# Gather rings of six and eight slots, a row-tiled spread, query and key gains ahead of the root, and new interleaving tables in a two-layer decoder step

## The reference, cut to what matters

```python
def peer_block(xt):                                # 128 tokens
    q = (xt @ w_q).reshape(128, 8, 2, 128)
    s1, s2 = q[:, :, 0] @ keys0.T, q[:, :, 1] @ keys1.T
    ...                                            # top 16 of the sums of two top 16: idx, top
    g = softmax(top)
    act = gelu(einsum('thkd,td->thk', u_tab[idx], xt))   # dots
    return einsum('thk,thkd->td', g * act, v_tab[idx])   # value sum

def mla_in(h, pos):                                # queries and keys of layer 0
    z = h @ w_in
    cq, ckv, kr = rms_norm(z[:256]), rms_norm(z[256:384]), z[384:]
    q = rope_tail(rms_norm((cq @ w_uq).reshape(8, 96), g_q), pos)
    k = rope_tail(rms_norm(concat(ckv @ w_uk, kr), g_k), pos)
```

## Time and profile before

| what | value |
| --- | --- |
| median of 3 runs | 2081.88 us (2077.25 to 2082.18) |
| the profiled execution, its own time | 2065.61 us |
| its span, first to last instruction | 2063.8 us |
| PE busy | 1503.8 us, 73% |
| DVE busy | 1321.5 us, 64% |
| POOL busy | 1203.5 us, 58% |
| data moved | 751.57 MB, 364 GB/s over the span |

### The profile page before, as it was taken

The page is one execution under the profiler, slowest core; times in us unless marked ns, Lnnn a source line. Parts: engine busy times, 40 slices in busy tenths (PEclk is TensorE's granted clock), DMA queues, the critical chain, the costliest instruction groups (busy, mean ns, idle before and its releaser), DMA issues.

```text
span 2063.8 us, 25764 instructions
## 1 busy us (share of the span) xinstructions
PE 1503.8 (73%) x9294; PEld 737.5 (36%) x9294; DVE 1321.5 (64%) x3189; ACT 355.2 (17%) x934; POOL 1203.5 (58%) x1097
## 2 busy tenths in 40 slices
PE   5775558774657869987886889978888871455667
PEld 2454223631233425552542447524543320111212
DVE  1459977699776645348889854478899417543452
ACT  1200122120121211111231311112122110011112
POOL 0023577476687564447767763457777437765575
PEclk8898788887767879898898888988888885678788
DMA  9859899999889999899999999899999889999999
GB/s 364 343 194 411 286 368 363 402 415 366 334 308 379 344 355 403 329 368 397 346 378 379 361 377 392 328 367 330 386 386 362 332 343 348 393 421 417 419 399 374
DMA packets 213942, 751.57 MB, mean 364 GB/s; under 512 B 27237, under 2 KB 35629, under 8 KB 213817
## 3 DMA queue, kind: packets, MB, share of 16 engines
q0 software_dynamic: 155136, 564.20, 71.3%
q1 hardware_dynamic: 58680, 185.72, 23.1%
HBM read 747.74 MB, written 2.10 MB: 363 GB/s over the span
## 4 chain that ended last, share of the span: by engine, by line
PE 24%; DVE 16%; DMA 13%; POOL 6%; issue 4%; ACT 1%; SPq 0%; POOLq 0%; DVEq 0%; ACTq 0%
PE yacc L1259 7%; DVE uring L2031 4%; DMA vring<-in_peer_v,expert 4%; POOL uring L798 3%; POOL vring L798 3%; DMA uring<-in_peer_u,expert 3%; DMA wring<-in_sg_w_in 3%; PE pp L1047 2%; PE pp L1021 2%; DMA wring<-in_peer_w_q 1%; DVE arena L1914 1%; PE pp L1110 1%; PE ps L1145 1%; PE pq L1110 1%; DMA wring<-in_sg_w_out 1%
## 5 line engine op out<-in xcount | busy, mean ns | idle before, releaser
L798 POOL DMA_INDIRECT uring<-in_peer_u,expert x512 | 577.0, 1127 | 462.2 <-DVE dots L2031 184.2
L1259 PE MATMUL yacc<-vring,diag 64*64 64x512 f32 x4096 | 621.9, 723 | 274.0 <-DMA vring<-in_peer_v,expert 147.9
L798 POOL DMA_INDIRECT vring<-in_peer_v,expert x512 | 553.9, 1082 | 355.2 <-PE yacc L1259 237.1
L2031 DVE CUSTOM_DVE_ANT_0 uring<-uring,h 128x1024 f32<-128x1024 f32 x512 | 613.7, 1225 | 205.3 <-DMA uring<-in_peer_u,expert 197.1
L1259 PEld LDWEIGHTS yacc<-vring,diag 64*64 64x64 f32 x4096 | 147.6, 154 | 606.5 <-issue 324.4
L1551 ACT ACTIVATE diag<-cst,wts 128x64 f32<-128x64 f32 (+1 forms) x528 | 155.4, 339 | 442.7 <-PE yacc L1259 367.2
L1047 PE MATMUL pp<-hT,wring 128*128 128x128 f32 x1024 | 128.2, 288 | 11.4 <-DMA wring<-in_peer_w_q 8.3
L1047 PEld LDWEIGHTS pp<-hT,wring 128*128 128x128 f32 x1024 | 124.0, 202 | 27.1 <-issue 16.4
L1914 DVE TENSOR_REDUCE arena<-arena 128x16 f32<-128x1024 f32 x64 | 77.9, 1217 | 20.8 <-ACT arena L1490 20.0
L1110 PE MATMUL pp<-w_uk,arena 128*128 128x512 f32 x128 | 76.8, 690 | 8.9 <-ACT arena L1490 8.9
L1111 PEld LDWEIGHTS ps<-qabs,arena 128*128 128x128 f32 x256 | 51.1, 200 | 66.4 <-issue 66.4
(11 more groups left out here) (306 smaller groups left out, 1824.3 us busy)
## 6 DMA issues: line engine op xcount, KB each, us to landing
wring<-in_peer_w_q SPq DMA_DIRECT2D x48, 1024.0 KB, 12.9
wring<-in_sg_w_in SPq DMA_DIRECT2D x48, 768.0 KB, 8.7
wring<-in_w_mod SPq DMA_DIRECT2D x35, 1024.0 KB, 9.5
wring<-in_sg_w_out SPq DMA_DIRECT2D x18, 1024.0 KB, 10.4
uring<-in_w_mod SPq DMA_DIRECT2D x9, 1024.0 KB, 11.9
wring<-in_mla_w_o SPq DMA_DIRECT2D x9, 1024.0 KB, 10.4
uring<-in_peer_u,expert POOLq DMA_INDIRECT x512, 7.1
vring<-in_peer_v,expert POOLq DMA_INDIRECT x512
```

Source lines behind the costliest of these rows:

```text
L798: pool.indirect_dma_start(ring[:, slot % RING, :], None, table[n // 3], bass.IndirectOffsetOnAxis(ap=idx, axis=0)).then_inc(land[slot % RI ...
L1259: last = pe.matmul(yacc[64 * q:64 * q + 64, r], diag[at, slot % RING, :], v[at, 512 * q:512 * q + 512], start=first, stop=final)
L2031: dve.tensor_tensor_reduce(u, u, rows_h[:, :], 1.0, 0.0, ALU.mult, ALU.add, dots[:, p % 2, i:i + 1]).then_inc(u_used, 1)
```

## The change

- `uring` gets 6 slots and `vring` 8; together they stay 14. The number of chunks loaded ahead stays six.
- `spread` reads only the 32 partitions of each quarter, so that a matmul takes a quarter of PE's rows. It runs in two turns; a turn takes quarters that lie in different row groups and writes different PSUM banks. Between the turns PE waits for the first turn's matmuls on a new semaphore. `norm` spreads its two rows together.
- `rsqrt_column` takes the place of `rsqrt` in `norm` and in the value norm of the sgu stages (`norm_v`). It is given minus half of the mean, and a round takes two instructions instead of three, so 8 in place of 11.
- In `mla_in` DVE now reads queries and keys from PSUM, multiplies them by the gains and rotates them before the root; ACT squares from PSUM at the same time and makes no copy. After the root one multiplication is left.
- All five tables are new. There are fewer spots on DVE, so the numbers aren't comparable one by one.

```diff
-RING = 7
+URING, VRING = 6, 8
 WRING = 4
-AHEAD = 2 * (RING // 2)
+AHEAD = 6
...
 PLAN_PE = """
-178:VV 179:NVVNNNNVNVV 180:VVV 181:VVVVV 186:V 189:VVV 191:V 193:VVVVV 194:V 200:VNV 206:VVVVVVV 209:VV 212:V 225:VV
...
+160:VVVVV 162:V 164:V 166:V 172:VVV 181:VVVV 187:V 190:VVV 191:V 192:VVVV 193:V 200:VV 205:V 206:VVVVVVV 209:VV 217:V
...
 PLAN_POOL = """
-UUUUUUVUUVVUUUUUVUUUVVUUUUUVUUUVVUVVUVVVUVVUVUVVVUUUUVVVUUUUUUUUVVVUUUUVVUVUVUUUVUUUVUVUUVVVUUVUUVUUUUUUVUUVUUUVUUUV
...
+UUUUUVUUVUVUUVUUUUUVUVVUUUVUUVVVUVVVUVUUVUUUVUVUUUUUVVUUUUUVUVVUUUVVUUVVVVUUVVVUUUUUUUUVVUUVVUUVUVVUUUVUUVUUUUUUVUUU
...
     if kind == "mla_in":
-        return ["z", "cT", "qk"], ["c", "kr", "qk"], ["z", "cT", "qk", "sq"]
+        return ["z", "cT", "qk"], ["c", "kr", "keys", "gain", "qk"], ["z", "cT", "queries", "sq"]
...
-            def gather(slot, ring, table, used, land):
+            def gather(slot, ring, size, table, used, land):
...
-                if slot >= RING:
-                    pool.wait_ge(used, slot - RING + 1)
+                if slot >= size:
+                    pool.wait_ge(used, slot - size + 1)
...
             def tables(k):
-                after(pe, ACTE, k - 1, "qk")
+                after(pe, ACTE, k - 1, "sq")
+                after(pe, DVE, k - 1, "gain")
...
-                spread(pp, mod_row(k) + 1)
-                signal(spread(pss, mod_row(k)), "rows")
+                signal(spread((pp, mod_row(k) + 1), (pss, mod_row(k))), "rows")
...
-            def spread(out, r):
-
-                pe.wait_ge(mod_done[DVE], mod_count(r))
-                for q in range(4):
-                    one = 32 * q + NT
-                    last = pe.matmul(out[:, q // 2, 256 * (q % 2):256 * (q % 2) + 256],
-                                     ident[:, one:one + 1].to_broadcast([P, P]), mrows[:, r, :], start=True, stop=True)
+            def spread(*rows):
+
+                for out, r in rows:
+                    pe.wait_ge(mod_done[DVE], mod_count(r))
+                for turn in range(2):
+                    for i, (out, r) in enumerate(rows):
+                        for bank in range(2):
+                            q = 2 * bank + (turn + i) % 2
+                            at, one = slice(32 * q, 32 * q + 32), 32 * q + NT
+                            last = pe.matmul(out[:, bank, 256 * (q % 2):256 * (q % 2) + 256],
+                                             ident[at, one:one + 1].to_broadcast([32, P]), mrows[at, r, :], start=True, stop=True)
+                            if turn == 0:
+                                last.then_inc(spread_half, 1)
+                                halves[0] += 1
+                    if turn == 0:
+                        pe.wait_ge(spread_half, halves[0])
                 return last
...
-                z, cT, qk, sq = (shape_of(tile, a, b) for a, b in ((z_, z_s), (cT_, cT_s), (qk_, qk_s), (sq_, sq_s)))
+                z, cT, sq = (shape_of(tile, a, b) for a, b in ((z_, z_s), (cT_, cT_s), (sq_, sq_s)))
                 after(act, PE, k, "z")
                 signal(copy(z[0:r, :], ps[0][0:r, 0:416]), "z")
                 point(k, 0)
                 after(act, PE, k, "cT")
                 signal(copy(cT[:, 0:3 * r], ps[1][:, 0:3 * r]), "cT")
+                keys = sq[0:r, 768:1536].rearrange("p (h d) -> p h d", h=H)
+                after(act, DVE, k, "kr")
+                act.activation(keys[:, :, NOPE:QK], krt[tile][0:r, :].unsqueeze(1).to_broadcast([r, H, ROPE]), ACT.Square)
                 after(act, PE, k, "qk")
-                copy(qk[0:r, 0:480], pp[0:r, 0, 0:480])
-                copy(qk[0:r, 480:768], pp[0:r, 1, 0:288])
-                keys = qk[0:r, 768:1536].rearrange("p (h d) -> p h d", h=H)
-                signal(copy(keys[:, :, 0:NOPE], ps[0][0:r, :].rearrange("p (h d) -> p h d", h=H)), "qk")
-                after(act, ACTE, k, "qk")
-                after(act, DVE, k, "kr")
-                signal(act.activation(sq[0:r, :], qk[0:r, :], ACT.Square), "sq")
+                act.activation(sq[0:r, 0:480], pp[0:r, 0, 0:480], ACT.Square)
+                signal(act.activation(sq[0:r, 480:768], pp[0:r, 1, 0:288], ACT.Square), "queries")
+                after(act, DVE, k, "keys")
+                signal(act.activation(keys[:, :, 0:NOPE], ps[0][0:r, :].rearrange("p (h d) -> p h d", h=H), ACT.Square), "sq")
...
-                if slot >= RING:
-                    act.wait_ge(v_used, slot - RING + 1)
+                if slot >= VRING:
+                    act.wait_ge(v_used, slot - VRING + 1)
...
+            def rsqrt_column(out, negative_half, tmp):
+
+                link(ts(out.bitcast(U32), negative_half.bitcast(U32), 1, None, ALU.logical_shift_right))
+                link(ts(out.bitcast(U32), out.bitcast(U32), -1.0, COLUMN_MAGIC, ALU.mult, ALU.add))
+                for _ in range(3):
+                    link(stt(tmp, out, out, negative_half, ALU.mult, ALU.mult))
+                    link(stt(out, tmp, 1.5, out, ALU.add, ALU.mult))
...
-                link(ts(scr[:, 0:1], ps[0][:, 0:1] if tile == S else scr[:, 0:1], 1.0 / D, EPS, ALU.mult, ALU.add))
-                rsqrt(scr[:, 1:2], scr[:, 0:1], rs[:, 0:1])
+                link(ts(scr[:, 0:1], ps[0][:, 0:1] if tile == S else scr[:, 0:1], -0.5 / D, -0.5 * EPS, ALU.mult, ALU.add))
+                rsqrt_column(scr[:, 1:2], scr[:, 0:1], rs[:, 0:1])
...
-                signal(cp(q4[:, 1, :, NOPE:QK], times(krt[tile][0:r, :], H)), "kr")
-                point(k, 0)
+                gq, gk = gqk[0:r, 0:QK], gqk[0:r, QK:2 * QK]
+                signal(tt(q4[:, 1, :, NOPE:QK], times(krt[tile][0:r, :], H), times(gk[:, NOPE:QK], H), ALU.mult), "kr")
+                point(k, 0)
+                after(dve, PE, k, "qk")
+                signal(tt(q4[:, 1, :, 0:NOPE], ps[0][0:r, :].rearrange("p (h d) -> p h d", h=H), times(gk[:, 0:NOPE], H),
+                          ALU.mult), "keys")
+                after(dve, ACTE, k, "queries")
+                link(tt(q4[:, 0, 0:5], pp[0:r, 0, 0:480].rearrange("p (h d) -> p h d", h=5), times(gq, 5), ALU.mult))
+                signal(tt(q4[:, 0, 5:8], pp[0:r, 1, 0:288].rearrange("p (h d) -> p h d", h=3), times(gq, 3), ALU.mult), "gain")
+                if tile == S:
+                    cos, sin = const("cos_q", r), const("sin_q", r)
+                else:
+                    cos, sin = (const(c)[:, HALF * tile:HALF * tile + HALF] for c in ("cos_p", "sin_p"))
+                link(rotate(q3[:, :, NOPE:QK], times(cos, 2 * H), times(sin, 2 * H), rt))
                 point(k, 1)
                 after(dve, ACTE, k, "sq")
                 s16, v16 = scr[0:r, 16:32], scr[0:r, 32:48]
                 link(dve.tensor_reduce(v16, sq.rearrange("p (i d) -> p i d", i=2 * H), X, ALU.add))
                 link(ts(v16, v16, 1.0 / QK, EPS, ALU.mult, ALU.add))
                 rsqrt(s16, v16, rs[0:r, 0:16])
-                link(tt(q3, q3, over(s16, QK), ALU.mult))
-                for i in range(2):
-                    link(tt(q4[:, i], q4[:, i], times(gqk[0:r, QK * i:QK * i + QK], H), ALU.mult))
-                if tile == S:
-                    cos, sin = const("cos_q", r), const("sin_q", r)
-                else:
-                    cos, sin = (const(c)[:, HALF * tile:HALF * tile + HALF] for c in ("cos_p", "sin_p"))
-                signal(rotate(q3[:, :, NOPE:QK], times(cos, 2 * H), times(sin, 2 * H), rt), "qk")
+                signal(tt(q3, q3, over(s16, QK), ALU.mult), "qk")
...
-                link(ts(scr[:, 0:1], squares, 0.25 / SGH, EPS, ALU.mult, ALU.add))
-                rsqrt(scr[:, 1:2], scr[:, 0:1], rs[:, 0:1])
+                link(ts(scr[:, 0:1], squares, -0.125 / SGH, -0.5 * EPS, ALU.mult, ALU.add))
+                rsqrt_column(scr[:, 1:2], scr[:, 0:1], rs[:, 0:1])
```

152 lines of the change are left out of this document (78 added, 74 removed).

## The result

The change made the kernel slower. Its median is 2095.9 us (2091.1 to 2102.4), against 2080.0 us (2077.1 to 2082.2) for the kernel before, run beside it, a ratio of 1.0103 with a 95% interval of 1.0078 to 1.0129. That is 16 us more where 15 us less were forecast. The profiled execution of the kernel after has a span of 2098.4 us. The one of before lies 14 us under its own median and this one 4 us above, so the 34.6 us between the two spans are more than twice the loss.

What follows compares the result with a forecast made beforehand. The prediction took the kernel as bound by data moved at 419 GB/s plus 270 us lost in slower stretches. Its terms summed to -14.5 us, carried over as -14.6 from the 2081.88 median to 2067 us, range 2045 to 2094.

Steps and rivals of the forecast that it cites:

- What bounds the kernel: Whole kernel: 270 us are lost where transfers run below 419 GB/s; the change moves the same data.
- Each microsecond taken out of it is one of the end: Start, 95 to 130 us: a latency chain on PE, ACT and DVE loses 28.3 us; time saved there shortens the whole.
- Spread, first norm: Start: four row tiles at once cut the spread to 2.3 us, so DVE starts 2.9 us sooner, between 0 and 3.7.
- the first rival: Row tiles don't overlap, or loads bound the start: about 2079 us, no change that can be told; chance 0.20.
- Projection and second norm: Start: a shorter projection spread gains 0.8 us, and an earlier spread and shorter root in the second norm 0.8 us.
- Gains ahead of the root: Attention input at the start: DVE ends some 4 us earlier, but PE's work hides it: 0, at most -2 us.
- First weights: After the sixth route: first value sum and freeing of vring come 4.2 us sooner, gaining 3 us, between 0 and 4.2.
- the slots behind POOL's head don't change this: At the first weights: one U slot less and one V more keep the same number in flight, leaving -3 us.
- Sgu stages: Both sgu passes: 6.4 us less PE work each, a third returning: -4 us for both, between 0 and -12.8.
- Ring sizes and tables: Gather waits: cost +13, gain down to -32, taken as -3 us; new tables unknown by 12 us either way.
- the rival of starved dots: Six slots make gathers for dots fall behind and POOL stop sooner: slower, 2094 us; chance 0.19.
- the 67 us: POOL's waits for dots: the most that one slot less could add, over 54 waits of 1.24 us.

## Why the prediction was wrong

**What bounds the kernel.** The reading of the holes was right, and so was "it can gain only by losing less". "Each microsecond taken out of it is one of the end" was only tried the other way, with work put in: at 12 us it holds within the interval, at 4 it can't be told.

**Spread, first norm (-2.9).** The mechanism was right and nearly the size: 2.6 us instead of 5.1, where 2.3 were forecast. The 0.3 and 0.7 us for the wait and for filling the array stood on no row; in the trace the second turn starts at 35.37, 0.14 us behind the first. `h` is at 36.76 instead of 38.09, only 1.3 us sooner, because the spread starts at 34.00 where it started at 32.88. Why is not shown. SyncE's new order issues one more chunk of conditioning weights ahead of `x`, but the kernels with its old order start the spread anywhere from 32.88 to 34.13, and those with the new one from 33.16 to 34.00. The whole-array spread varied too, from 3.7 us at a granted clock of 1.00 (the rings alone) to 6.4 us at 0.54 (seven and eight slots, old tables). The rule that a change of tiling mode drains the array (the Trainium skill, TensorEngine Tiling (Array Packing), Key Properties) spoke for the first rival. The trace doesn't agree that it takes the gain: the tiles overlap, and PE is idle for 1.21 us ahead of the spread, which waits for `mrows`, where it was 1.10 on the whole array. In the second layer a norm's spread begins at 889.84 us while the value sums on 64*64 tiles end at 889.90.

**What became of it (the step that failed at the start).** I carried the gain to the first gather. In the whole change it never arrived: 143.16 us, not 136.3. Two things stand between. PE awaits a chunk in front of attention at about 77 us, in five of the eight kernels with the whole new code for 3.6 to 4.8 us (2.2 to 3.3 in the others), where the earlier trace rows has 2.87. And PE's clock in the stretch behind it differs from kernel to kernel. The stretch from 80 to 95 us, after, and then before:

```profile
80.00:95.00 15.00, 12.46 (x110) 8.34 (x108) 7.33 (x14) 6.38 (x22) 0.00 (x0) 0.82 1.03 415
```

```profile
80.00:95.00 15.00, 12.12 (x120) 8.19 (x121) 7.33 (x14) 6.37 (x22) 0.00 (x0) 1.00 0.99 387
```

Five of the 18 traces whose start wasn't lengthened have a granted clock under 0.9 there, and these five have the first gather at 143.0 to 144.1 us; the other thirteen have it at 139.6 to 142.5. One of the five has nothing new but the short roots, one nothing new but `mla_in`. So the start's gain of 1.3 us was smaller than what goes with the clock behind the awaited chunk, 2.5 us between the means of the two groups, and the forecast had no term for that. Why the chunk is awaited longer with the new `mla_in` is not settled.

**Projection and second norm (-0.8, -0.8).** From the projection's spread to the second norm's `h` it was 22.3 us and is 21.4, so 0.95 of the 1.6 came. It is spent by the first gather, which comes 44.25 us after that spread and came 44.24 us after it before. The traces show on what. The transposes and the query matmuls behind the second norm, and the clock there, before:

```profile
120.45 0.66 PE L855 MATMUL ps<-cst,h 128*128 128x128 f32 x4 [1.65 <-DVE h L1671]
...
123.50 5.44 PE L1047 MATMUL pp<-hT,wring 128*128 128x128 f32 x32 [0.89 <-ACT hT L1302]
```

```profile
120.00:124.00 4.00, 1.81 (x12) 1.37 (x13) 1.83 (x3) 1.19 (x2) 0.00 (x0) 1.00 0.00 0
```

And after:

```profile
121.82 1.12 PE L859 MATMUL ps<-cst,h 128*128 128x128 f32 x4 [3.13 <-DVE h L1692]
...
125.33 5.93 PE L1060 MATMUL pp<-hT,wring 128*128 128x128 f32 x32 [0.89 <-ACT hT L1315]
```

```profile
120.00:124.00 4.00, 1.80 (x7) 1.40 (x8) 3.09 (x6) 0.60 (x1) 0.00 (x0) 0.50 0.00 0
```

The shorter spread leaves PE idle for 3.13 us instead of 1.65 ahead of the transposes. These run at a granted clock of 0.50 instead of 1.00, the second four end 0.46 us later behind `h`, and the query matmuls take 0.49 us more: together the 0.95 us. All nine kernels with the tiled spread show it (idle for 2.1 to 3.1 us, then 1.1 us for four transposes at 0.50); of the nine with the old spread eight are idle for 1.64 or 1.65 us and take 0.65 or 0.66, and the ninth takes 1.11 us for the second four. So the time that the second norm's spread saved was given back in PE's clock, a term that the forecast lacked. That the longer idle time makes the clock fall is what the traces suggest; they don't show it apart from the spread's tiles.

**Gains ahead of the root (0).** Right: 1.0014 (0.9977 to 1.0051) by itself.

**First weights (-3).** The value sum came 4.3 us sooner, where this term said 4.2, and the stretch moved less, not more. I counted the slots in flight and left out which gather stands at GpSimd's head. The head was a value gather whose ring was full, for 10.71 us. The sentence that failed is "the slots behind POOL's head don't change this".

**Sgu stages (-4).** The spreads there are shorter (1.6 us instead of 3.7 in a norm), and PE's busy time fell from 93.25 to 91.44 us in the second stage with the new code alone, and the time didn't: 1.0010 for all the new code, 0.9999 for the spread. No run shows a gain of 4 us or its absence; the interval of the former is 5 us wide on each side. As the whole code sums to 2 us more (-4 to 7), and the forecast gave its parts 8.5 us less, the sum of these terms was too high by at least 5 us.

**Ring sizes and tables (-3, the term that sank it).** It was one number for two things. The rings alone cost 35 us at the old tables, where the rival of starved dots gave a share of the 67 us; measured, that share is about half. The sign that I named for it, waits for dots that grow, came with the rings alone and not in the kernel after (185.4 us, and 184.2 before). The new tables seem to take some 10 us of it back (in two pairs of overlapping intervals), and they bring a cost that stays when the slot is given back: 0.85%, 18 us, with seven and eight. The rival's mechanism is shown for the old tables, by the runs with six and eight, six and seven, and by the hole at 1460 us. In the kernel after it is not what costs, since the seventh slot gives nothing back. So the rival came near the time (2094 against 2096) partly by luck, by an argument that holds for the old tables. "That new tables of this length are otherwise as good as the old ones I can't read from rows" named the weak place, and 12 us either way was too little where 18 were needed.

What stays open: which of the orders makes the rest beside SyncE's, some 10 us. GpSimd's and the three compute engines' belong together, and no run parts them further. No version in these runs beats the kernel before; the nearest, the short roots alone, is at 0.9983 with an interval that holds 1.

## What to carry to other kernels

Where one engine issues two kinds of transfers in a fixed order, a ring's depth has no price of its own. Ask what stands at the head of that order when the slots run out, and what is queued behind it: one slot less for the dots cost 1.4 to 1.7% with the old tables and nothing that can be told with the new ones, one slot more cost up to 0.55%, and GpSimd's old order cost 3% in the company of the other new ones. The total of a wait is no price: 285 us of waits for dots came with no loss in one kernel, and 333 us with 35 us in another. A table that was laid out for one set of buffers must be judged with them, and a change of both must be costed as two.

Before a gain of a microsecond or two is carried through a chain, look at what varies behind it: an awaited load and the granted clock after it went with first gathers up to 4.6 us apart, and the gain was 1.3. And where a saving leaves the engine idle for longer, read the granted clock behind it: here what a shorter spread had saved went to matmuls at half the clock.

## What was not expected of the hardware

The same kernel before took 2071 to 2080 us in four sessions, and 2176 and 2195 us in two others, 5 to 6% more. The record numbers the chips of the five sessions of experiments 0, 3, 1, 0 and 1. So the session of 2195 us and the last one, of 2073 us, have the same number, and the chip is not shown to be the reason. The fastest stretches are alike: from 1900 to 2000 us the run with seven and eight slots and old tables moved 419 GB/s in the slowest session. From 400 to 1600 us it moved 341 GB/s, where before's profile has 365. What makes it so stays open.

Row tiles of 32 rows ran four at a time on matmuls of 256 columns: 16 records in 2.6 us at a granted clock of 0.50 (33 to 37 us of the kernel after), and in 1.6 us at 1.00 (116 to 119 us), the wait between the two turns included. On the whole array they had taken 5.1 us at 0.72 and 3.7 us at 1.00. One trace doesn't fit: in the run with the new code alone the spread at 33.24 us took 2.6 us as well, and the clock stands there at 1.00.
